# Mixer stage of a hybrid RWKV-7 / Mamba-2 step: one fence taken out on three engines, three parts re-ordered, one scale on ScalarE

## The reference, cut to what matters

```python
kk = heads(k * k_k)
kk = kk / jnp.maximum(jnp.sqrt(jnp.sum(kk * kk, axis=-1, keepdims=True)), 1e-12)
k_mod = heads(k * (1.0 + (a - 1.0) * k_a))
a_vec, b_vec = -kk, kk * ah
def step(S, inp):                       # one token, state S is [value, key] per head
    sa = einsum('bhvk,bhk->bhv', S, a_t)
    S = S * w_t + sa * b_t + v_t * k_t
    return S, einsum('bhvk,bhk->bhv', S, r_t)
...
# Mamba-2, after its scan and the gate silu(z):
yg = y.reshape(bsz, t, M_GROUPS, M_WIDTH // M_GROUPS)
yg = yg * lax.rsqrt(jnp.mean(yg * yg, axis=-1, keepdims=True) + NORM_EPS)
y = yg.reshape(bsz, t, M_WIDTH) * norm_w
```

## Time and profile before

| | us |
|---|---|
| median of 3 runs | 2652.03 |
| lowest and highest | 2647.5, 2655.84 |
| the profiled execution | 2649.54 |
| its span on the core | 2647.6 |
| TensorE busy in the span | 2449.5 (93%) |
| VectorE busy | 1520.1 (57%) |
| ScalarE busy | 949.3 (36%) |
| GpSimd busy | 642.8 (24%) |
| mean granted clock of TensorE | 0.954 of full speed |

### The profile page before, as it was taken

How to read it: one execution, slowest core, us unless ns; L and a number is a source line. 1 busy time by engine, 2 the same in 40 slices (tenths; PEclk the granted TensorE clock), 3 DMA queues, 4 the chain that set the end, 5 groups by cost and what they waited for, 6 DMA issues and landing times. The chain is left out here.

```text
span 2647.6 us, 50323 instructions
## 1 busy us (share of the span) xinstructions
PE 2449.5 (93%) x20078; PEld 2386.9 (90%) x20078; DVE 1520.1 (57%) x2792; ACT 949.3 (36%) x1802; POOL 642.8 (24%) x314
## 2 busy tenths in 40 slices
PE   7987788878989899899989999999999999999997
PEld 6985677777989898888889999999999999999997
DVE  4344554533877865888735444544544544777774
ACT  4234444223323233888842222223222222222221
POOL 2433443422454444111122112112212210000000
PEclk9997988769989999999989999999999999999999
DMA  4331000031322232666663233233223322555551
GB/s 176 121 102 54 26 26 14 2 118 50 99 91 95 80 103 96 177 176 177 190 227 125 97 113 115 89 108 109 105 100 105 115 97 81 172 186 167 175 175 41
DMA packets 162460, 296.02 MB, mean 112 GB/s; under 512 B 11872, under 2 KB 99232, under 8 KB 158120
## 3 DMA queue, kind: packets, MB, share of 16 engines
q1 hardware_dynamic: 162344, 294.38, 33.7%
HBM read 230.03 MB, written 64.31 MB: 111 GB/s over the span
## 5 line engine op out<-in xcount | busy, mean ns | idle before, releaser
L123 PE MATMUL banks<-w_high,v_low 128*128 128x288 f32 x2048 | 604.5, 295 | 0.0
L121 PE MATMUL banks<-w_high,v_high 128*128 128x288 f32 x2048 | 603.6, 295 | 0.4
L122 PE MATMUL banks<-w_low,v_high 128*128 128x288 f32 x2048 | 603.1, 294 | 0.0
L121 PE MATMUL banks<-res_hi,u_high 128*128 128x288 f32 x1440 | 428.1, 297 | 10.9 <-ACTq L2097 10.9
L123 PE MATMUL banks<-res_hi,u_low 128*128 128x288 f32 x1440 | 425.4, 295 | 0.0
L122 PE MATMUL banks<-res_lo,u_high 128*128 128x288 f32 x1440 | 425.1, 295 | 0.0
L121 PEld LDWEIGHTS banks<-w_high,v_high 128*128 128x128 f32 x2048 | 384.2, 188 | 3.7 <-DVE w_low L2067 3.7
L122 PEld LDWEIGHTS banks<-w_low,v_high 128*128 128x128 f32 x2048 | 384.1, 188 | 0.0
L123 PEld LDWEIGHTS banks<-w_high,v_low 128*128 128x128 f32 x2048 | 384.1, 188 | 0.0
L2091 DVE TENSOR_TENSOR res_x<-banks,res_x 128x288 f32<-128x288 f32 x512 | 225.1, 454 | 267.2 <-PE banks L123 267.2
L1713 POOL TENSOR_TENSOR u_low<-u_raw,u_high 128x1024 fp32r<-128x1024 f32 x72 | 183.5, 2550 | 706.1 <-ACT u_high L1709 706.1
(11 more groups left out here) (338 smaller groups left out, 4301.4 us busy)
## 6 DMA issues: line engine op xcount, KB each, us to landing
v_raw<-arg_v SPq DMA_DIRECT2D x128, 512.0 KB, 3.8
scratch_gates<-gate_stage SPq DMA_DIRECT2D x18, 2048.0 KB, 9.3
u_raw<-arg_u SPq DMA_DIRECT2D x36, 1024.0 KB, 5.8
gates_in<-scratch_gates SPq DMA_DIRECT2D x32, 1152.0 KB, 7.2
q_raw<-arg_u SPq DMA_DIRECT2D x38, 512.0 KB, 3.6
scratch_hidden<-gelu_ahead SPq DMA_DIRECT2D x56, 288.0 KB, 2.5
gelu_out<-scratch_hidden SPq DMA_DIRECT2D x56, 288.0 KB, 2.8
in_raw<-arg_w_in SPq DMA_DIRECT2D x25, 512.0 KB, 3.8
```

Of the source, the lines that this page charges most:

```text
L121: pe.matmul(out, ah, bh, start=first, stop=False)
L122: pe.matmul(out, ah, bl, start=False, stop=False)
L123: return pe.matmul(out, al, bh, start=False, stop=last)
```

## The change

Six edits, all in the mixer:

1. TensorE, ScalarE and GpSimd no longer call `b_fence` ahead of B1. VectorE still does.
2. Part S3 (the rk scores, with their take on ScalarE and their mask on GpSimd) stands right behind B1, ahead of L1, and no longer behind Y3 in L3. The wait for the take of r_hatT goes with it.
3. VectorE makes b_hat and k_hat in a new part A3b behind A4 and C4 in L4, ahead of the masks of L5. They were the end of A3 in L3. A semaphore `k_scaled` links the two halves.
4. In VectorE's B1 the two s_mid_pairs products stand behind the inverse's start (lines 1317 and 1318) instead of ahead of the masks.
5. The scale of y_mamba by the inverse root is two ScalarE activations (one per group) at the end of L5, ahead of L6, in place of one GpSimd multiply. GpSimd waits for them before it multiplies by the weights.
6. The PSUM jobs follow the new order of parts.

```diff
--- before.py
+++ after.py
@@ -513,11 +513,11 @@
 
 
 def tile_parts():
-    parts = [(name, 0) for name in ("A1", "A2", "A2b", "A3", "A4", "A5")]
-    between = {1: ("C1", "Y1", "S1", "A1"), 2: ("C2", "A2", "Y2", "A2b", "S2"), 3: ("C3", "A3", "Y3", "S3"),
-               4: ("A4", "C4"), 5: ("A5",)}
+    parts = [(name, 0) for name in ("A1", "A2", "A2b", "A3", "A4", "A3b", "A5")]
+    between = {1: ("C1", "Y1", "S1", "A1"), 2: ("C2", "A2", "Y2", "A2b", "S2"), 3: ("C3", "A3", "Y3"),
+               4: ("A4", "C4", "A3b"), 5: ("A5",)}
     for i in range(NT):
-        parts.append(("B1", i))
+        parts += [("B1", i), ("S3", i)]
         for n in range(1, last_level(i) + 1):
             parts.append((f"L{n}", i))
             for name in between.get(n, ()):
@@ -672,6 +672,8 @@
         xdt_rdy = core.sem("xdt_ready")
         rk_rdy = core.sem("rkT_ready")
         kmod = core.sem("k_mod_ready")
+        kscaled = core.sem("k_scaled")
+        yscaled = core.sem("mamba_scaled")
         knorm_in, knorm = core.sem("key_norm_arg"), core.sem("key_norm")
         mnorm_in, mnorm = core.sem("mamba_norm_arg"), core.sem("mamba_norm")
         gnorm_in, gnorm = core.sem("group_norm_arg"), core.sem("group_norm")
@@ -861,7 +863,6 @@
                     return ins
 
                 def b1(i, tok, T, rc, xc):
-                    b_fence(pe, i)
                     for n, (name, src) in enumerate((("bT", bh2[:, i % 2]), ("kT", kh2[:, i % 2]), ("aT", ah), ("rT", rh))):
                         pe.wait_ge(hats, 4 * i + n + 1)
                         o = b.start(pe, name, i)
@@ -887,10 +888,10 @@
                     scores("ak", i, T, kT, aT)
 
                 def s2(i, tok, T, rc, xc):
+                    scores("rb", i, T, bT, rT)
+
+                def s3(i, tok, T, rc, xc):
                     b.wait_taken(pe, "rT", i)
-                    scores("rb", i, T, bT, rT)
-
-                def s3(i, tok, T, rc, xc):
                     scores("rk", i, T, kT, rT)
 
                 def level(n):
@@ -1069,7 +1070,6 @@
                         act.activation(sg, sg, ACT.Exp).then_inc(seg_exp, 1)
 
                 def b1(i, tok, T, rc, xc):
-                    b_fence(act, i)
                     for name, dst in (("bT", bT), ("kT", kT), ("aT", aT), ("rT", rT)):
                         take(name, i, dst[:, :, 0:T], 4 * T)
                     for e in range(2):
@@ -1106,6 +1106,11 @@
                         if n == 4:
                             act.wait_ge(mnorm_in, i + 1)
                             act.activation(msmall[0:T, 3, 0:2], msmall[0:T, 2, 0:2], ACT.Sqrt).then_inc(mnorm, 1)
+                        if n == 5:
+                            act.wait_ge(yinv, i + 1)
+                            for g in range(2):
+                                y = ym[0:T, 4 * g:4 * g + 4, :]
+                                act.activation(y, y, ACT.Copy, scale=msmall[0:T, 1, g:g + 1]).then_inc(yscaled, 1)
                     return run
 
                 def b5(i, tok, T, rc, xc):
@@ -1167,7 +1172,6 @@
                     TT(xw2[0:T, i % 2], xdt2[0:T, i % 2], per_head(ecs2[0:T, i % 2, 1, :], T), ALU.mult).then_inc(xdt_rdy, 1)
 
                 def b1(i, tok, T, rc, xc):
-                    b_fence(pool, i)
                     for e in range(2):
                         b.wait_taken(pool, f"m{e}", i)
                         x = inv[0:T, e, 0]
@@ -1192,9 +1196,7 @@
                     TT(t2[0:T], ym[0:T], ym[0:T], ALU.mult).then_inc(ysq, 1)
 
                 def l5(i, tok, T, rc, xc):
-                    pool.wait_ge(yinv, i + 1)
-                    yg = ym[0:T].rearrange("p (g h) d -> p g (h d)", g=2)
-                    link(TT(yg, yg, bc(msmall[0:T, 1, 0:2], 2, [T, 2, 4 * HD]), ALU.mult))
+                    pool.wait_ge(yscaled, 2 * (i + 1))
                     TT(ym[0:T], ym[0:T], row(7, T), ALU.mult).then_inc(om_rdy, 1)
 
                 def b5(i, tok, T, rc, xc):
@@ -1270,7 +1272,10 @@
                     link(TS(small[0:T, 2, :], small[0:T, 1, :], 1e-12, None, ALU.max))
                     link(dve.reciprocal(small[0:T, 3, :], small[0:T, 2, :]))
                     link(TT(kk[0:T], kk[0:T], per_head(small[0:T, 3, :], T), ALU.mult))
-                    link(TT(t0[0:T], kk[0:T], h3(wa[0:T, 1, :]), ALU.mult))
+                    TT(t0[0:T], kk[0:T], h3(wa[0:T, 1, :]), ALU.mult).then_inc(kscaled, 1)
+
+                def a3b(i, tok, T, rc, xc):
+                    dve.wait_ge(kscaled, i + 1)
                     b.wait_taken(dve, "cinc", i)
                     TT(h3(bh2[0:T, i % 2, :]), t0[0:T], eneg[0:T], ALU.mult).then_inc(hats, 1)
                     TT(h3(kh2[0:T, i % 2, :]), km[0:T], eneg[0:T], ALU.mult).then_inc(hats, 1)
@@ -1302,12 +1307,6 @@
 
                 def b1(i, tok, T, rc, xc):
                     b_fence(dve, i)
-
-                    for e in range(2):
-                        es = slice(e * HD, (e + 1) * HD)
-                        TT(s0d[es, :, e, :], st[es, frm[i]], bc(dec2[es, i % 2, :, 0], 2, [HD, 4, HD]),
-                           ALU.mult).then_inc(s0d_rdy, 1)
-
                     for e in range(2):
                         in_blocks(f"ab{e}", i, T, mT[0:T, e], C_MSB)
                     for e in range(2):
@@ -1316,6 +1315,10 @@
                     for e in range(2):
                         link(TT(mT[0:T, e], mT[0:T, e], block_mask(C_IDB, T), ALU.add))
                         TT(inv[0:T, e, 1], mT[0:T, e], block_mask(C_LTB, T), ALU.mult).then_inc(xt_rdy, 1)
+                    for e in range(2):
+                        es = slice(e * HD, (e + 1) * HD)
+                        TT(s0d[es, :, e, :], st[es, frm[i]], bc(dec2[es, i % 2, :, 0], 2, [HD, 4, HD]),
+                           ALU.mult).then_inc(s0d_rdy, 1)
 
                 def masked(name, i, T, dst, mask):
                     for e in range(2):
@@ -1391,7 +1394,7 @@
                     if i == NT - 1:
                         scale_outputs(dve, link, i, T)
 
-                run_parts({"A1": a1, "A2": a2, "A2b": a2b, "A3": a3, "A4": a4, "A5": a5, "Y1": y1, "Y2": y2, "Y3": y3, "B1": b1, "S1": s1, "S2": s2, "B5": b5, "C1": c1, "C3": c3,
+                run_parts({"A1": a1, "A2": a2, "A2b": a2b, "A3": a3, "A3b": a3b, "A4": a4, "A5": a5, "Y1": y1, "Y2": y2, "Y3": y3, "B1": b1, "S1": s1, "S2": s2, "B5": b5, "C1": c1, "C3": c3,
                            **{f"L{n}": level(n) for n in range(1, LEVELS)}})
 
 
```

More of the change, by code:

```diff
@@ L889, in s2 @@
                 def s2(i, tok, T, rc, xc):
-                    b.wait_taken(pe, "rT", i)
                     scores("rb", i, T, bT, rT)
                 def s3(i, tok, T, rc, xc):
+                    b.wait_taken(pe, "rT", i)
                     scores("rk", i, T, kT, rT)
```

## The result

| | before | after |
|---|---|---|
| median of 9 runs each, us | 2647.5 | 2664.06 |
| lowest and highest | 2643.14, 2655.84 | 2659.17, 2674.95 |
| the profiled execution | 2649.54 | 2667.97 |

The ratio is 1.0061, with a 95% interval of 1.0045 to 1.0078. The forecast was 2645.4 us, 0.25% under the 2652.03 that it started from, range 2635 to 2656 us; the measured median lies above it.

The account below looks back on a forecast made before the run. TensorE was taken to bound the kernel, so only idle or half-clock time inside the mixer could move. The terms -6.3 + 10.0 + 0.3 - 8.2 - 3.0 + 0.6 gave -6.6 us: 2645.4 us, range 2635 to 2656.

Parts of the forecast that it names:

- the sum's term for B5: B5 to its last product, in all five tiles: forecast to change by 0 us.
- the third rival: Idle time ahead of level 5's x brings the clock down in B5; three more slow tiles, +7.8 us, 2659.8; chance 0.15.
- The sign that I named for the clock: Forecast wrong if the clock's share in the mixer moves by more than 0.03 from 0.80.
- The fence: At four tile starts TensorE's 1.57 us of idle time go: -6.3 us.
- B1: the price: Rk masks and s_mid_pairs delay level 1's x products by 2.5 us in tiles 0 to 3: +10.0 us.
- The choice of alternation over line 1197's example: In B1 VectorE and GpSimd take turns, +2.5 us per tile, though line 1197 let three VectorE operations go first.
- b_hat and k_hat: Moved behind A4: level 4 starts 3.24 us earlier, 1.19 us paid ahead of level 5; four tiles, -8.2 us.
- The clock's own term at level 4: Level 4's x products run faster after shorter idle time: half of 1.5 us per tile, -3.0 us.
- rk in tile 4: Taking the rk products off TensorE's path in tile 4's L3 at half clock saves 0.9 us.
- The scale on ScalarE: Between the takes of level 5 and L6: 0.6 us for two, +0.15 in four tiles, +0.6 us.
- no turns are lost in B1: VectorE gets its port in B1 whenever it asks, or GpSimd comes late: sum -14.8 us, 2637.2; chance 0.30.
- b_hat and k_hat only move the wait: GpSimd still works when they run, so level 5 gives back level 4's gain: +1.6 us, 2653.6; chance 0.13.

Follow-up runs that it names:

- idle time filled: Changed kernel with 14 extra, unused 128x128 matmuls on TensorE ahead of level 5's first x product in full tiles: 1.0006 of the kernel before.
- edit 1 alone: Kernel before with only the fence ahead of B1 removed on TensorE, ScalarE and GpSimd: 0.9958 of the kernel before.
- edits 1 and 3: Kernel before with the fence removed on three engines and b_hat and k_hat moved behind A4 and C4: 0.9977 of the kernel before.
- edits 1 and 5: Kernel before with the fence removed on three engines and the scale of y_mamba on ScalarE: 1.0014 of the kernel before.
- edit 4 undone: Changed kernel with the two s_mid_pairs products ahead of B1's masks again: 1.0023 of the kernel before.
- edits 3 and 5 undone: Changed kernel with b_hat and k_hat back at the end of A3 and the y_mamba scale back on GpSimd: 0.9995 of the kernel before.
- edit 2 undone: Changed kernel with the rk scores, takes and masks back in L3: 1.0024 of the kernel before.
- edit 5 undone: Changed kernel with GpSimd scaling y_mamba again: 1.0039 of the kernel before.
- edit 3 undone: Changed kernel with b_hat and k_hat back at the end of A3, ahead of the level 4 masks: 1.0082 of the kernel before.

## Why the prediction was wrong

**The clock ahead of B5, wrong, and it decides the case.** The step that failed is the sum's term for B5, put at nothing, on the argument that full TensorE work between level 4 and level 5 keeps the clock up. The mechanism stands in the forecast as the third rival, with its place and its price of 3.8 us per tile, and it is what happened: +17.9 us, of which tiles 0, 1 and 3 gave 12.1, against the 11.4 written down, and tile 2, already slow before, 5.8 more. I gave it 0.15 because the segments' and transposes' products lie between level 4 and level 5. They did not protect what comes after them: the idle time ahead of level 5's x stands behind them, and then come the join's products, which wait for ScalarE's takes. Each edit was priced by whether it delays something. None was priced by what its idle time does to the clock of the work behind it. Before, B5 of tile 2 had already shown the fall without any help, at 0.72; of four tiles, one at the edge should have stood for a likely case. The sign that I named for the clock would not have warned either: over the mixer it moved only from 0.80 to 0.79, since what B5 lost, level 4 and tile 4 partly gave back.

```profile
200.00:560.00 360.00, 290.90 (x3947) 257.38 (x3949) 169.45 (x340) 149.01 (x291) 123.33 (x109) 0.79 0.08 22
```

The period from tile 1 to tile 2, forecast to fall by about 2 us from 66.30, rose to 72.72.

**The fence: right.** No idle time ahead of the transposes, 1.57 us in four tiles.

**B1: the price right, the sum in part by luck.** +5.1 against +4.9 for the whole stretch, but tile 1 gave +2.2 and tiles 2 and 3 next to nothing, where the forecast had +0.9 in each. Tile 1's transposes came to run at the lower level; those of tiles 2 and 3 already did before, and took 10.3 and 10.2 us to level 1's x against tile 1's 8.5, so the tiles were not alike here. Where the clock was up for all but the end of the stretch, 11.2 us (idle time filled, tiles 1 to 3) stand against 8.7 (edit 1 alone), so 2.5 us, the price taken. Without the rk masks 2 to 3 us go, without s_mid_pairs 1.0 to 1.4; they overlap, since the masks also slow the pairs. The choice of alternation over line 1197's example was right here; line 1317 and both s_mid_pairs waited. The Trainium skill ("SBUF — State Buffer", section "Who interferes with whom"), by whose rule the one that issues first goes first, gave +10.8 for it, and the trace agrees in B1: 1.37 and 1.71 us. It does not cover line 1197's 3.21 us.

**b_hat and k_hat: right in tiles 1 to 3, wrong in tile 0.** "Four tiles are alike" failed: in tile 0 no group norm of an older tile runs on GpSimd, the two products took 0.69 and 0.68 us there before too, and the move gained nothing (-0.1 with the clock, against -2.8). The clock's own term at level 4, half of 1.5 us, held in sum: tile 1 stayed at the lower level, with 1.11 us for the first group, tiles 2 and 3 rose. In tiles 0 to 3 -9.1 against -11.2.

**rk in tile 4: right, with a gift of the clock beside it.** There rk stood behind level 3's x (519.01 us) and ahead of level 4's, so its 0.9 belongs to the stretch to level 5's x. With tile 4 at the lower level that stretch took 13.18 us with rk in L3 (kernel before, edits 1 and 3, edits 1 and 5) and 12.33 to 12.37 without it (edit 4 undone, edits 3 and 5 undone, idle time filled): 0.8 us. The -3.2 us ahead of level 3's x are the clock alone: 14.5 us in all six of these kernels, wherever rk stands, and 11.3 in the changed one, where part of it ran at 2.4 GHz, as with edit 2 undone (11.5).

**The scale on ScalarE: mis-sized.** The pair took 0.91 us, not 0.6, and it lengthened the stretch from level 5's x to B5 by 0.64 us even at full clock, not 0.15. ScalarE's timeline in tile 1 of the changed kernel:

```profile
352.15 0.91 ACT L1113 ACTIVATE y_mamba<-y_mamba,msmall 128x256 f32<-128x256 f32 x2
353.08 0.65 ACT L1097 ACTIVATE level<-banks 64x256 f32<-64x256 f32 x2
```

The first L6 take had to wait for it, and the second, behind it, was late as well. I had let the second go free.

**The other rivals.** That no turns are lost in B1 was refuted by the same rows. That b_hat and k_hat only move the wait holds when GpSimd has the rk masks in L4 (1.75 us for k_hat with edits 1 and 3 alone), not in the full change, where both took 0.68 and 0.69.

## What to carry to other kernels

An idle microsecond on TensorE can cost more than itself where the granted clock already moves from tile to tile: price every wait by the clock of the stretch behind it, and look in the profile before for a tile in which that has already happened. When work must leave one wait's path, put it behind the last mask that anything waits for and not ahead of the next one. Of the same two products, placed ahead of level 5's masks and behind them, the first gave 0.9977 and the second 0.9894. Before moving an elementwise multiply on GpSimd, look at what VectorE does there with two SBUF operands.

## What the runs showed of the hardware

- Where the clock fell decides what B5 loses. In all the traces, where it fell between 0.6 us ahead of B5's first product and that product itself, it stayed down to the end of B5: 21.3 us for the products that take 11.8, five tiles, TensorE busy 20.6 us of them at a granted 0.50. Where it fell 0.6 to 6.7 us ahead it came back inside B5, which took 16.1 to 16.4 us (twelve tiles); where it fell 0.2 to 0.6 us behind the first product, 15.6 to 15.9 us (seven tiles). The Trainium skill ("TensorE: Matmul & The Clock Gate", section "HAM oscillation — how this bites in real kernels") describes the clock falling in waits and the work behind running slow. The trace agrees on that much; a busy TensorE that stays at the lower level for 20 us is beyond what I had read from it.
- Idle times of 2.0 to 2.5 us ahead of level 5 were enough without the longer join (edit 5 undone, three of four tiles), and so was a join longer by 0.6 us without them (edit 3 undone, three of four; edits 1 and 5 alone, two of four).
- How often it falls differs between tiles with the same instructions (edits 1 and 5 alone: B5 11.8, 15.8, 11.8, 16.2 us). What decides it within one kernel I did not settle; with edits 1 and 3 alone it is worth up to 20 us between two runs of one kernel (2637.5 to 2657.61).
- A matmul of 128x128 in f32 against 128 columns leaves two records and takes about 0.24 us: 14 of them 3.39 us.
